# A decoder layer's down projection in 32 steps over a sliding range of contraction pairs

## The chip, the cores and the metric

The kernel runs on one core of a Trainium2 chip. The metric is the device time of one execution in microseconds (us). The kernel before took 3311.81 us (median of 3 runs, 3308.32 to 3328.85).

A core has a matrix engine (TensorE, PE in the profile, with its weight loads as PEld), VectorE (DVE), ScalarE (ACT), GpSimd (POOL) and SyncE (SP). SP here only issues DMAs; ACT and POOL issue some as well. Each engine takes its own instructions in order, and engines wait for one another by semaphores.

## The reference: what is computed

One layer of a hybrid decoder for 592 tokens (64 sample tokens, 16 meta tokens, 512 prompt tokens), D_MODEL 2048, all in float32:

```python
h = rmsnorm(x, norm1_w)
mix = token_mixer(h, ...)            # w_in projection, two groups of recurrent heads, w_out projection
x = x + mix
u = relu(rmsnorm(x, norm2_w) @ w_up) # 2048 -> 8192
x = x + (u * u) @ w_down             # 8192 -> 2048
y = rmsnorm(x, final_norm_w)
```

The change touches the last product alone, `(u * u) @ w_down`, for the 576 tokens that are returned (the meta tokens are dropped before it).

## The kernel before, in words

**Split numbers.** Every float32 operand is split into a high part (rounded to the matrix engine's fast float32 form by an ACT copy) and a low part (the rest, by a DVE subtraction). A product is three matrix products: high weights by high data, high by low, low by high.

**Seven products in place of eight.** The two MLP projections take the 576 tokens as 2 halves of TH = 288, output columns as pairs of 128-wide tiles and contraction rows as pairs. One 2 by 2 by 2 block product is made from 7 products (`FORMS`) of sums and differences of the four blocks of each side. A *pair* p is a pair of output tiles with 7 products, each over KP = 8 contraction pairs with 3 matmuls apiece: 24 matmuls of 288 columns per product, 168 per pair. The up projection has 32 pairs (p = 0 to 31), the down projection another 32 (p = 32 to 63).

**The data side of the down projection.** The squared activations of up pair q are contraction pair q of the down projection. They and their sums and differences (8 planes of 128 by 288) are made in `ub`, stored by GpSimd to the DRAM tensor `u_forms` (`store_u`, L762), and later read back. Only 8 contraction pairs fit on chip: `forms_a` (forms 0 to 2) and `forms_b` (forms 3 to 6) hold a high and a low part of each form for 8 contraction pairs.

**Four chunks.** The down projection therefore runs in 4 chunks of 8 contraction pairs. In each chunk all 8 output pairs are visited; each visit reads the output's running sum `z` from DRAM, adds its 7 products (`take`, L2180) and stores it again (`store_z`, L767). Ahead of each chunk all 7 forms are loaded anew: ACT issues one DMA of 1152 KB per form (`form_load`, L1587), turns it into the high part (`chunk_hi`, L1592) and DVE makes the low part in two halves (`chunk_lo`, L2227). This is spread over the slots of the pair before the chunk and the chunk's first pair.

**The order of the work.** It is written out by hand. Each engine runs through slots (p, i), i = 0 to 6. In slot i, DVE first adds a finished product (`take` of product i-2), then makes the low part of the weights of product i (`mlp_lo`, L2172), and in slots 1, 3, 5 and 6 one weight sum (`weight_sum`, L2137; those of slots 5 and 6 are for the next pair). ACT makes the high part of the weights of product i+1 (`mlp_hi`, L1538). TensorE waits at the head of product i for the low part of its weights (`product_waits`, L1187).

**The weights.** A pair needs 4 weight blocks of 512 KB (j = 0 to 3). SP issues them in order (`load_block`, L524) into a ring of 6, each when its place comes free; the running sums `z` go through the same queue (`load_z`, L543). Blocks 2 and 3 of a pair are needed first: the sum of the two is what DVE makes in slot 5 of the pair before. The fourth block (j = 3) is issued after the weight sum of slot 3, two slots ahead of that.

Of the kernel before, what the change touches and what calls it, by code (L numbers as in the profile page):

```python
# [21 lines left out]
F32 = mybir.dt.float32  # L22
# [6 lines left out]
P = 128  # L29
# [39 lines left out]
UB = [0, 4, 6, 3, 5, 2, 7]  # L69
BLOCK_AT = [2, 3, 0, 1, 4, 5]  # L70
DVE_FORMS = list(range(FORMS))
# [31 lines left out]
def next_form_chunk(p):  # L103

    return (p + 1 - UP_PAIRS) // KP if p + 1 >= UP_PAIRS and (p + 1 - UP_PAIRS) % KP == 0 and p + 1 < PAIRS else None

def this_form_chunk(p):
    return (p - UP_PAIRS) // KP if p >= UP_PAIRS and (p - UP_PAIRS) % KP == 0 else None
# [79 lines left out]
def hymba_kernel(nc, io):  # L189
    ctx = ExitStack()  # L190
    with ctx:
# [10 lines left out]
        u_dram = nc.dram_tensor("u_forms", [CHUNKS, FORMS + 1, P, KP, TH], F32, kind="Internal").ap()  # L202
# [106 lines left out]
        with ExitStack() as s:  # L309
# [10 lines left out]
            sb("plane_rest", [P, KP * TH - UK * P - 4 * TH], stack=s)  # L320
            with ExitStack() as s2:
                ub = sb("ub", [P, 2, FORMS + 1, TH], stack=s2)
            with ExitStack() as s2:
                z = sb("z", [P, 2, 4, TH], stack=s2)
                zsq = sb("zsq", [P, 2, TN], stack=s2)
                zacc = sb("zacc", [P, TN], stack=s2)
                fin = sb("fin", [P, NW], stack=s2)
            sb("ub_rest", [P, 2, FORMS + 1, TH], stack=s)
            w_raw2 = sb("w_raw2", [P, 2, UK, P], stack=s)

# [88 lines left out]
        s_fraw = [sem(f"form_loaded{i}") for i in range(FORMS)]  # L419
        s_tc = sem("product_copied")  # L420
# [41 lines left out]
        def _(sp):  # L462
# [61 lines left out]
            def load_block(n):  # L524
# [52 lines left out]
        def _(pool):  # L577
# [184 lines left out]
            def store_u(p):  # L762
                pool.wait_ge(s_uf, 3 * p + 3)
                pool.dma_start(u_dram[p // KP][:, :, p % KP, :].rearrange("f p n -> p f n"),
                               ub[:, p % 2]).then_inc(s_ust[p % 2], 16)

            def store_z(p):  # L767
# [3 lines left out]
                else:  # L771
                    e = d - KP * (CHUNKS - 1)
                    for r in range(2):
                        pool.wait_ge(s_zq, 2 * e + r + 1)
                        if e == 0 and r == 0:
                            pool.tensor_copy(zacc[:, :], zsq[:, 0, :]).then_inc(s_zacc, 1)
                        else:
                            pool.wait_ge(s_zacc, 2 * e + r)
                            pool.tensor_tensor(zacc[:, :], zacc[:, :], zsq[:, r, :], ALU.add).then_inc(s_zacc, 1)
# [51 lines left out]
        def _(pe):  # L831
# [341 lines left out]
            def part_product(p, i, ks):  # L1173
# [3 lines left out]
                out = pbank(p, "abacaba"[i])  # L1177
                for k in ks:
                    if p == 0 and i < 3:
                        pe.wait_ge(s_flo, form_no(f"{i}_{k}"))  # L1180
                    for n, (w, x) in enumerate(((hi_slot(u_), f_hi), (hi_slot(u_), f_lo), (w_lo[:, u_ % 2], f_hi))):
                        ins = mm(out, w[:, k, :], x[:, k, :], start=i in (0, 1, 3) and k == 0 and n == 0,  # L1182
# [4 lines left out]
            def product_waits(p, i):  # L1187
# [75 lines left out]
        def _(act):  # L1263
# [274 lines left out]
            def mlp_hi(p, i):  # L1538
# [5 lines left out]
                else:  # L1544
                    n_ = 4 * p + {0: 0, 3: 1, 6: 3}[i]
                    act.wait_ge(s_v[n_ % BLOCKS], 16 * (n_ // BLOCKS + 1))
# [7 lines left out]
            def copy_product(p, n):  # L1554

                i, dst = ((0, 0), (1, 2), (2, 1))[n]
# [8 lines left out]
            def u_square(p, n):  # L1565
# [6 lines left out]
                A(ub[:, p % 2, 2 * n:2 * n + 2, :], part[:, 2 * n:2 * n + 2, :], ACT.Square).then_inc(s_sqr, 1)  # L1572

            def z_finish(p, r):
# [3 lines left out]
                if e == 0 and r == 0:  # L1578
# [744 lines left out]
```

## Time and profile before

| | us |
|---|---|
| runs: median (lowest, highest) | 3311.81 (3308.32, 3328.85) |
| profiled execution, whole | 3322.78 |
| its span, first to last instruction | 3321.2 |
| TensorE busy | 3040.7 (92%) |
| VectorE busy | 2014.2 (61%) |
| ScalarE busy | 1189.7 (36%) |
| starts of the first and last matmul of the up and down products (L1182) | 1762.6 and 3299.2 |

The mean granted clock of TensorE was 0.96 of full speed. The page divides the span into 40 slices of 83 us; the MLP starts in slice 22. A row of the chain of waits gives a start, a length and the work that held up the end at that moment; a row of the timeline gives start, length, engine, line and operation, and in brackets the idle time before it and what ended it.

### The profile page before, as it was taken

Reading aid. Unit: us, or ns where it says so; the run is one execution under the profiler, and the core shown is the slowest. Engines: PE = TensorE matmul, PEld = TensorE weight load, DVE = VectorE, ACT = ScalarE, POOL = GpSimd, SP = SyncE. Lnnn points to the kernel's source line nnn. Section 1 sums busy time; section 2 is a strip of 40 time slices with the busy share of each in tenths; the row PEclk is TensorE's granted clock in tenths of the full one; section 3 lists DMA queues with packets and bytes.
Section 4 is the critical chain, followed back from the end, with each engine's and each line's share of the span. In section 5 each row is a group of like instructions: output and inputs, shape, how many; then the busy total and the mean of one; then the engine's idle time right before and its main releaser. Section 6 shows DMA issues by size and latency. Waiting matters only on the chain.

```text
span 3321.2 us, 54780 instructions
## 1 busy us (share of the span) xinstructions
PE 3040.7 (92%) x22024; PEld 2973.4 (90%) x22024; DVE 2014.2 (61%) x2800; ACT 1189.7 (36%) x1481; POOL 315.5 (9%) x432
## 2 busy tenths in 40 slices
PE   5999999898989898986999999999998989899798
PEld 4998988898989898875999999999997979899798
DVE  3546363645454463644447777777768777677775
ACT  3333232232323232332334444444443343333443
POOL 4010101010201011010110000000000000000021
PEclk8999999999999999997999999999999989999999
DMA  7544334542344457952433444444465565645655
GB/s 163 75 66 68 61 71 53 57 74 56 70 64 68 63 67 55 68 107 65 126 108 104 153 153 139 153 153 146 139 210 159 150 205 150 208 140 150 204 146 178
DMA packets 481058, 385.65 MB, mean 116 GB/s; under 512 B 15296, under 2 KB 446992, under 8 KB 477216
## 3 DMA queue, kind: packets, MB, share of 16 engines
q1 hardware_dynamic: 453936, 260.60, 39.2%
q0 software_dynamic: 22832, 88.39, 7.4%
q10 hardware_dynamic: 4032, 33.03, 2.6%
q8 instruction: 184, 3.01, 0.4%
q14 instruction: 74, 0.61, 0.1%
HBM read 297.65 MB, written 84.33 MB: 115 GB/s over the span
## 4 chain that ended last, share of the span: by engine, by line
PE 77%; DVE 10%; issue 6%; ACT 4%; DMA 2%; SPq 0%; DVEq 0%; POOL 0%; ACTq 0%
PE main L1182 34%; PE main L839 26%; PE mx L1182 6%; PE mx L1084 2%; PE mx L983 1%; PE mx L991 1%; PE mx L915 1%; PE mx L899 1%; DVE w_lo L2178 1%; DVE w_lo L1677 1%; DVE forms_b L2231 1%; DMA w_raw<-in_w_in 1%; ACT w_hi L1277 1%; DMA w_raw<-in_w_down 1%; PE mx L942 1%
## 5 line engine op out<-in xcount | busy, mean ns | idle before, releaser
L839 PE MATMUL main<-h_hi,w_hi 128*128 128x296 f32 (+1 forms) x2592 | 627.7, 324 | 81.7 <-DVE w_lo L1677 47.3
L1182 PE MATMUL main<-forms_b,w_hi 128*128 128x288 f32 x3072 | 624.7, 298 | 57.3 <-DVE w_lo L2178 43.1
L1182 PE MATMUL main<-forms_a,w_hi 128*128 128x288 f32 x3072 | 619.3, 297 | 14.6 <-DVE forms_a L2231 10.6
L839 PE MATMUL main<-h_lo,w_hi 128*128 128x296 f32 (+1 forms) x2592 | 579.5, 306 | 0.0
L839 PE MATMUL main<-h_hi,w_lo 128*128 128x296 f32 (+1 forms) x2592 | 577.2, 305 | 0.0
L1182 PEld LDWEIGHTS main<-forms_b,w_hi 128*128 128x128 f32 x3072 | 500.4, 191 | 60.8 <-DVE w_lo L2178 44.7
L839 PEld LDWEIGHTS main<-h_hi,w_hi 128*128 128x128 f32 x2592 | 429.8, 197 | 97.2 <-issue 52.3
L1182 PEld LDWEIGHTS main<-forms_a,w_hi 128*128 128x128 f32 x3072 | 498.0, 190 | 16.8 <-issue 16.6
L1182 PE MATMUL main<-forms_a,w_lo 128*128 128x288 f32 x1536 | 457.2, 298 | 0.0
L1182 PE MATMUL main<-forms_b,w_lo 128*128 128x288 f32 x1536 | 456.8, 297 | 0.0
L839 PEld LDWEIGHTS main<-h_lo,w_hi 128*128 128x128 f32 x2592 | 436.6, 196 | 0.0
L839 PEld LDWEIGHTS main<-h_hi,w_lo 128*128 128x128 f32 x2592 | 435.6, 195 | 0.0
L1552 ACT ACTIVATE w_hi<-w_raw 128x1024 fp32r<-128x1024 f32 x256 | 271.2, 1059 | 387.0 <-PE main L1182 251.2
L2178 DVE TENSOR_TENSOR w_lo<-w_raw,w_hi 128x1024 fp32r<-128x1024 f32 x256 | 312.3, 1220 | 65.3 <-PE main L1182 65.3
L1552 ACT ACTIVATE w_hi<-w_sum 128x1024 fp32r<-128x1024 f32 x190 | 201.4, 1060 | 340.6 <-PE main L1182 304.1
L1182 PEld LDWEIGHTS main<-forms_b,w_lo 128*128 128x128 f32 x1536 | 293.7, 191 | 0.0
L1182 PEld LDWEIGHTS main<-forms_a,w_lo 128*128 128x128 f32 x1536 | 291.0, 189 | 0.0
L1677 DVE TENSOR_TENSOR w_lo<-w_raw,w_hi 128x1024 fp32r<-128x1024 f32 x162 | 197.5, 1220 | 141.4 <-ACT w_hi L1272 97.3
L2178 DVE TENSOR_TENSOR w_lo<-w_sum,w_hi 128x1024 fp32r<-128x1024 f32 x190 | 233.8, 1231 | 16.6 <-PE main L1182 16.6
L1182 PE MATMUL mx<-forms_b,w_hi 128*128 128x288 f32 x1024 | 209.7, 298 | 8.0 <-DVE forms_b L2231 8.0
L1277 ACT ACTIVATE w_hi<-w_raw 128x1024 fp32r<-128x1024 f32 x112 | 117.8, 1052 | 241.3 <-PE main L839 241.3
L2191 DVE TENSOR_TENSOR z<-z,main 128x288 f32<-128x288 f32 x192 | 87.0, 453 | 144.7 <-PE main L1182 144.5
(375 smaller groups left out, 3715.1 us busy)
## 6 DMA issues: line engine op xcount, KB each, us to landing
w_raw<-in_w_in SPq DMA_DIRECT2D x130, 512.0 KB, 8.3
w_raw<-in_w_up SPq DMA_DIRECT2D x128, 512.0 KB, 4.0
w_raw<-in_w_down SPq DMA_DIRECT2D x128, 512.0 KB, 4.7
u_forms<-ub POOLq DMA_DIRECT2D x32, 1152.0 KB, 6.6
forms_b<-u_forms ACTq DMA_DIRECT2D x16, 1152.0 KB, 7.7
z<-x_scratch SPq DMA_DIRECT2D x32, 576.0 KB, 7.6
x_scratch<-z POOLq DMA_DIRECT2D x31, 576.0 KB, 3.1
w_raw<-in_w_out SPq DMA_DIRECT2D x32, 512.0 KB, 4.2
```

The costliest lines, as they stand in the source:

```text
L839: ins = mm(out[:, half, :], w[:, ring, k, :], x[:, kx, half * width:half * width + width], start=first and n == 0, stop=last_ and n == 2)
L899: ins = mm(mx[:, i + half, 0:HALF], ones[:, :], src[:, half * HALF:half * HALF + HALF], start=True, stop=True)
L915: ins = pe.transpose(mxf[:, 512 * i + n_ * P:512 * i + n_ * P + P], src(c), ident[:, :])
L942: ins = mm(mx[:, 2 * i + half, 0:HALF], ones[0:16, :], sel[i][:, half * HALF:half * HALF + HALF], start=True, stop=True)
L983: ins = mm(bank(0, 64 * c, 64), xl[:, c, :], left, start=True, stop=True)
L1084: ins = mm(bank(i % 2, 64 * c, 64), win(hkk, c), hqq[:, ctok(c):ctok(c) + 64], start=True, stop=True)
L1182: ins = mm(out, w[:, k, :], x[:, k, :], start=i in (0, 1, 3) and k == 0 and n == 0, stop=k == KP - 1 and n == 2, skip_group_check=True)
L1277: A(w_hi[:, ring % 2], w_raw[:, ring], ACT.Copy).then_inc(s_hi, 1)
L1552: A(hi_slot(u_), src, ACT.Copy).then_inc(s_hi, 1)
L1677: TT(w_lo[:, ring % 2], w_raw[:, ring], w_hi[:, ring % 2].bitcast(F32), ALU.subtract).then_inc(s_lo, 1)
L2178: TT(w_lo[:, u_ % 2], src, hi_slot(u_).bitcast(F32), ALU.subtract).then_inc(s_lo, 1)
L2191: TT(o[:, q, :], o[:, q, :], src, ALU.add).then_inc(s_ev, 1)
```

## The change

The down projection is no longer in 4 chunks but in 32 steps t = 0 to 31. Step t still makes the 7 products of output pair t mod 8 over 8 contraction pairs, but these are t to t+7, taken modulo 32. So each output pair is visited 4 times, and its four ranges together cover all 32 pairs once. From one step to the next a single contraction pair leaves the range and one comes in. Its 7 forms (3 for `forms_a`, 4 for `forms_b`) overwrite the place of the one that left.

- The first fill (7 forms of 8 pairs) is issued by SP (`load_form`), among the weight blocks, no longer by ACT.
- The other three fills of all forms are gone. Each of steps 1 to 31 has two loads issued by ACT (`step_load`: 3 planes, then 4 planes), into a buffer `stage` (for step 1 straight into the forms), two ACT copies for the high parts (`step_hi`), and two DVE subtractions for the low parts (`step_lo`).
- TensorE waits for them in the middle of a product: in products 0 and 3 of a step, ahead of the last of the 8 contraction pairs.
- `u_forms` is stored by contraction pair, so that the 3 planes and the 4 planes each lie together; the planes in `ub` have another order for it, and with them some slices of ACT and DVE in the up projection.
- From step 25 on the range wraps round, and a weight block is loaded by two DMAs in place of one.
- `zsq` and `zacc` move onto `part` and `rstd` to make room for `stage`.

```diff
@@ sync (SP) @@
-                    c, m = (p - UP_PAIRS) // KP, 2 * ((p - UP_PAIRS) % KP) + j // 2
-                    src = w_down[:, KT * c + j % 2:KT * c + KT:2, m * P:m * P + P]
+                    m = 2 * ((p - UP_PAIRS) % KP) + j // 2
+                    q, i = window(p)[0], 0
+                    while i < KP:
+                        n_ = min(KP - i, UP_PAIRS - q)
+                        src = w_down[:, 2 * q + j % 2:2 * (q + n_ - 1) + j % 2 + 1:2, m * P:m * P + P]
+                        sp.dma_start(wblock(n)[:, i:i + n_, :], src).then_inc(s_v[n % BLOCKS], 16)
+                        q, i = 0, i + n_
+                    return
...
+            def load_form(i):
+
+                sp.wait_ge(s_unit, unit_of(UP_PAIRS - 1, i) + 1)
+                sp.wait_ge(s_ust[0], 16 * (KP // 2))
+                sp.wait_ge(s_ust[1], 16 * (KP // 2))
+                sp.dma_start(form(i)[1].bitcast(F32), u_dram[0:KP, UB[i]].rearrange("k p n -> p k n")).then_inc(s_fraw[i], 16)
...
+                for i in {4 * UP_PAIRS + 2: (0, 1), 4 * UP_PAIRS + 4: (2,)}.get(n, ()):
+                    load_form(i)
                 if p >= UP_PAIRS:
                     load_z(p)
+                for i in {4 * UP_PAIRS + 4: (3, 4), 4 * UP_PAIRS + 5: (5, 6)}.get(n, ()):
+                    load_form(i)
@@ tensor (PE) @@
+                t = p - UP_PAIRS
                 for k in ks:
+                    if t > 0 and k == KP - 1 and i in (0, 3):
+                        pe.wait_ge(s_flo, step_forms(t, i // 3))
...
+                    kx = k if t < 0 else window(p)[k] % KP
...
-                c = this_form_chunk(p)
-                if c is not None:
-                    if i in DVE_FORMS:
-                        pe.wait_ge(s_flo, len(F_ORDER) + len(DVE_FORMS) * c + DVE_FORMS.index(i) + 1)
+                if p == UP_PAIRS:
+                    pe.wait_ge(s_flo, len(F_ORDER) + i + 1)
@@ scalar (ACT) @@
-            def form_load(c, i):
-                act.wait_ge(s_ust[0], 16 * (KP // 2) * (c + 1))
-                act.wait_ge(s_ust[1], 16 * (KP // 2) * (c + 1))
-                act.dma_start(form(i)[1].bitcast(F32), u_dram[c, UB[i]]).then_inc(s_fraw[i], 16)
...
+            def step_load(t, group):
+
+                q = (t + KP - 1) % UP_PAIRS
+                i0, i1 = (4, 8) if group else (0, 3)
+                act.wait_ge(s_ust[q % 2], 16 * (q // 2 + 1))
+                src = u_dram[q, i0:i1].rearrange("f p n -> p f n")
+                if t == 1:
+                    dst = (forms_b if group else forms_a)[:, :, 1, q % KP, :].bitcast(F32)
+                else:
+                    dst = stage[:, i0:i1, :]
+                    if t == 2:
+                        act.wait_ge(s_ust[1], 16 * (UP_PAIRS // 2))
+                    else:
+                        act.wait_ge(s_flo, step_forms(t - 1, group))
+                act.dma_start(dst, src).then_inc(s_step[group], 16)
+
+            def step_hi(t, group):
...
+                act.wait_ge(s_step[group], 16 * t)
+                act.wait_ge(s_unit, unit_of(UP_PAIRS + t - 1, 6 if group else 2) + 1)
+                A(f[:, :, 0, q, :], f[:, :, 1, q, :].bitcast(F32) if t == 1 else stage[:, i0:i1, :], ACT.Copy).then_inc(s_fhi, 1)
...
+                if t > 1 and i == 1:
+                    step_hi(t, 1)
+                if 0 < t < STEPS - 1:
+                    if i == 0:
+                        step_load(t + 1, 0)
+                    if i == 3:
+                        step_load(t + 1, 1)
+                    if i == 4:
+                        step_hi(t + 1, 0)
@@ vector (DVE) @@
+            def step_lo(t, group):
+                q = (t + KP - 1) % KP
+                f = forms_b if group else forms_a
+                dve.wait_ge(s_fhi, step_forms(t, group))
+                lo_ = f[:, :, 1, q, :]
+                TT(lo_, lo_.bitcast(F32) if t == 1 else stage[:, 4:8, :] if group else stage[:, 0:3, :],
+                   f[:, :, 0, q, :].bitcast(F32), ALU.subtract).then_inc(s_flo, 1)
...
+                if t > 1 and i == 2:
+                    step_lo(t, 1)
+                if 0 < t < STEPS - 1 and i == 4:
+                    step_lo(t + 1, 0)
```

**SP's queue at the first fill.** These are SP's DMAs from the blocks of the first down pair on (L541 or L562: a weight block; L551 or L582: a running sum; L572: one form of the fill), before:

```order
L541 DMA w_raw<-in_w_down 128x8x128 [waits weights_lo] x2
L541 DMA w_raw<-in_w_down 128x8x128 [waits weight_sum_made] x2
L541 DMA w_raw<-in_w_down 128x8x128 [waits weights_lo]
L551 DMA z<-x_scratch 128x1152 [waits x1_stored1,x1_stored0,u_stored0]
L541 DMA w_raw<-in_w_down 128x8x128 [waits weights_lo]
L541 DMA w_raw<-in_w_down 128x8x128 [waits weight_sum_made] x2
```

and now:

```order
L562 DMA w_raw<-in_w_down 128x8x128 [waits weights_lo] x2
L562 DMA w_raw<-in_w_down 128x8x128 [waits weight_sum_made]
L572 DMA forms_a<-u_forms 128x8x288 [waits u_stored1,u_stored0,unit_done] x2
L562 DMA w_raw<-in_w_down 128x8x128 [waits weight_sum_made]
L562 DMA w_raw<-in_w_down 128x8x128 [waits weights_lo]
L572 DMA forms_a<-u_forms 128x8x288 [waits u_stored1,u_stored0,unit_done]
L582 DMA z<-x_scratch 128x1152 [waits x1_stored1,x1_stored0,u_stored0]
L572 DMA forms_b<-u_forms 128x8x288 [waits u_stored1,u_stored0,unit_done] x2
L562 DMA w_raw<-in_w_down 128x8x128 [waits weights_lo]
L572 DMA forms_b<-u_forms 128x8x288 [waits u_stored1,u_stored0,unit_done] x2
L562 DMA w_raw<-in_w_down 128x8x128 [waits weight_sum_made] x2
```

The fourth block of the first down pair now stands behind two forms, and the third and fourth block of the second down pair behind all seven; before, no form was in this queue.

**DVE in one step of the new down projection** (slots 2 to 5 of a step; L2255 adds a product, L2242 makes a low part of weights, L2233 and L2216 are weight sums, L2304 is `step_lo`):

```order
L2255 TENSOR_TENSOR z<-z,main 128x288 [waits z_loaded0,unit_done]
L2242 TENSOR_TENSOR w_lo<-w_sum,w_hi 128x1024 [waits unit_done,weights_hi]
L2304 TENSOR_TENSOR forms_b<-stage,forms_b 128x4x288 [waits form_hi]
L2255 TENSOR_TENSOR z<-z,main 128x288 [waits unit_done]
L2242 TENSOR_TENSOR w_lo<-w_raw,w_hi 128x1024 [waits unit_done,weights_hi]
L2233 TENSOR_TENSOR w_sum<-w_raw,w_sum 128x1024 [waits weights_lo,weight_sum_made,block_loaded1]
L2255 TENSOR_TENSOR z<-z,main 128x288 [waits unit_done]
L2242 TENSOR_TENSOR w_lo<-w_raw,w_hi 128x1024 [waits unit_done,weights_hi]
L2304 TENSOR_TENSOR forms_a<-stage,forms_a 128x3x288 [waits form_hi]
L2255 TENSOR_TENSOR z<-z,mx 128x288 [waits product_taken,unit_done]
L2242 TENSOR_TENSOR w_lo<-w_sum,w_hi 128x1024 [waits unit_done,weights_hi]
L2216 TENSOR_TENSOR w_sum<-w_raw 128x1024 [waits weight_sum_made,weights_lo,block_loaded1,block_loaded0]
```

The two subtractions stand in slots 2 and 4, the slots of the down projection that had no weight sum besides slot 0. Apart from them a step has the same DVE instructions as a pair inside a chunk had.

## Rows read from the trace of the kernel before

**Rows 1.** The page: busy time by engine

```profile
PE 3040.7 (92%) x22024; PEld 2973.4 (90%) x22024; DVE 2014.2 (61%) x2800; ACT 1189.7 (36%) x1481; POOL 315.5 (9%) x432
```

**Rows 2.** Chain of waits, 2440 to 3321 us: start, length, work

```profile
2452.12 3.20 PE mx L1182 x24
...
2546.27 3.20 PE mx L1182 x24
...
2657.75 3.21 PE mx L1182 x24
...
2748.82 3.22 PE mx L1182 x24
...
2860.32 3.19 PE mx L1182 x24
...
2953.02 3.19 PE mx L1182 x24
...
3064.54 3.19 PE mx L1182 x24
...
3153.00 3.19 PE mx L1182 x24
...
3286.80 3.20 PE mx L1182 x24
```

**Rows 3.** Timeline of DVE, 2455 to 2545 us

```profile
2456.85 1.22 DVE L2152 TENSOR_TENSOR w_sum<-w_raw 128x1024 f32<-128x1024 f32 x1
...
2458.55 0.45 DVE L2201 TENSOR_TENSOR part<-part,main 128x288 f32<-128x288 f32 x1 [0.47 <-PE main L1182]
...
2478.00 1.22 DVE L2178 TENSOR_TENSOR w_lo<-w_sum,w_hi 128x1024 fp32r<-128x1024 f32 x1
2493.81 1.23 DVE L2152 TENSOR_TENSOR w_sum<-w_raw 128x1024 f32<-128x1024 f32 x1 [14.60 <-issue]
...
2495.32 1.22 DVE L2178 TENSOR_TENSOR w_lo<-w_raw,w_hi 128x1024 fp32r<-128x1024 f32 x1
...
2524.24 1.22 DVE L2152 TENSOR_TENSOR w_sum<-w_raw 128x1024 f32<-128x1024 f32 x1
...
2533.45 1.21 DVE L2178 TENSOR_TENSOR w_lo<-w_raw,w_hi 128x1024 fp32r<-128x1024 f32 x1
2536.76 0.45 DVE L2191 TENSOR_TENSOR z<-z,main 128x288 f32<-128x288 f32 x1 [2.10 <-PE main L1182]
```

**Rows 4.** SP: timeline from 2470 us; landing of L541's DMA issued 2471 to 2475

```profile
2473.70 2.43 SPq L541 DMA_DIRECT2D w_raw<-in_w_down  x2
...
DMA to landing us min/median/max: 20.0/20.0/20.0
```

**Rows 5.** Timeline of DVE, then of ACT, inside a chunk, 2562 to 2586 us

```profile
2565.39 0.45 DVE L2191 TENSOR_TENSOR z<-z,main 128x288 f32<-128x288 f32 x1 [1.57 <-PE main L1182]
...
2571.78 0.46 DVE L2191 TENSOR_TENSOR z<-z,mx 128x288 f32<-128x288 f32 x1 [1.53 <-PE mx L1182]
...
2568.65 1.07 ACT L1552 ACTIVATE w_hi<-w_sum 128x1024 fp32r<-128x1024 f32 x1 [2.14 <-PE main L1182]
```

**Rows 6.** All uses of L2231, then of the copies L1595: min/median/max in ns

```profile
L2231 DVE TENSOR_TENSOR forms_b<-forms_b x32: 1346/1349/1354, 2515.3 to 3138.5; 128x1152 fp32r<-128x1152 f32 x32
...
L1595 ACT ACTIVATE forms_b<-forms_b x16: 2107/2115/2125, 2504.3 to 3124.9; 128x2304 fp32r<-128x2304 f32 x16
```

**Rows 7.** One pair by engine (busy PE, PEld, DVE, ACT, POOL; clock, DMA share, GB/s)

```profile
2562.30:2584.60 22.30, 22.30 (x171) 22.30 (x170) 15.77 (x19) 7.47 (x8) 0.53 (x1) 1.00 0.51 148
```

**Rows 8.** DMA issues in 2570 to 2592 us: KB each, median us to landing

```profile
w_raw<-in_w_down SPq DMA_DIRECT2D x4, 512.0 KB, 4.8
```

**Rows 9.** Landing of all 28 form loads, L1590

```profile
DMA to landing us min/median/max: 5.1/9.3/12.1
```

**Rows 10.** DMA totals in 1560 to 1580 us, then in 1568 to 1576 us

```profile
DMA packets 7726, 5.48 MB, mean 274 GB/s; under 512 B 2025, under 2 KB 7662, under 8 KB 7726
...
DMA packets 3241, 2.71 MB, mean 339 GB/s; under 512 B 832, under 2 KB 3241, under 8 KB 3241
```

More of the change, by code:

```diff
@@ L100, in out_done, with window, block_loads, block_count @@
     return OUT_U0 + (3 + m if m < 2 else 2 * m + 2)
[L103 to L109, printed above, removed]
+STEPS = PAIRS - UP_PAIRS
+FIRST_FORMS = len(F_ORDER) + FORMS
+def window(p):
+    return [(p - UP_PAIRS + i) % UP_PAIRS for i in range(KP)]
+def block_loads(n):
+    p = n // 4
+    return 2 if p >= UP_PAIRS and p - UP_PAIRS + KP > UP_PAIRS else 1
+def block_count(n):
+    return 16 * sum(block_loads(m) for m in range(n % BLOCKS, n + 1, BLOCKS))
+def step_forms(t, group):
+    return FIRST_FORMS + 2 * (t - 1) + 1 + group
 def w0(c):
@@ L324, in hymba_kernel @@
                 z = sb("z", [P, 2, 4, TH], stack=s2)
-                zsq = sb("zsq", [P, 2, TN], stack=s2)
-                zacc = sb("zacc", [P, TN], stack=s2)
-                fin = sb("fin", [P, NW], stack=s2)
+                stage = sb("stage", [P, FORMS + 1, TH], stack=s2)
             sb("ub_rest", [P, 2, FORMS + 1, TH], stack=s)
             w_raw2 = sb("w_raw2", [P, 2, UK, P], stack=s)
+        zsq = part[:, :, :].rearrange("p (a b) n -> p a (b n)", a=2)
+        zacc = rstd[:, 0:TN]
         def x1_tile(m):
@@ L419, in hymba_kernel @@
         s_fraw = [sem(f"form_loaded{i}") for i in range(FORMS)]
+        s_step = [sem(f"step_forms_loaded{i}") for i in range(2)]
         s_tc = sem("product_copied")
@@ L1571, in u_square @@
                         act.wait_ge(s_ust[p % 2], 16 * (p // 2))
-                A(ub[:, p % 2, 2 * n:2 * n + 2, :], part[:, 2 * n:2 * n + 2, :], ACT.Square).then_inc(s_sqr, 1)
+                A(ub[:, p % 2, (4 if n else 0):(7 if n else 4):(2 if n else 3), :], part[:, 2 * n:2 * n + 2, :], ACT.Square).then_inc(s_sqr, 1)
             def z_finish(p, r):
@@ L1577, in z_finish @@
                 act.wait_ge(s_ev, ev_no(p, 6 + r))
-                if e == 0 and r == 0:
-                    act.wait_ge(s_ust[1], 16 * (UP_PAIRS // 2))
                 if e:
@@ L1609, in slot @@
                         z_finish(p - 1, i)
[L1610 to L1621 removed]
+                t = p - UP_PAIRS
+                if t == -1 and i >= 5:
+                    chunk_hi(i - 5)
+                if t == 0 and i < 5:
+                    chunk_hi(i + 2)
+                if t == 0 and i == 4:
+                    step_load(1, 0)
+                if t == 0 and i == 6:
+                    step_hi(1, 0)
+                if t == 1 and i == 1:
+                    step_load(1, 1)
+                if t == 1 and i == 2:
+                    step_hi(1, 1)
+                if t > 1 and i == 1:
[7 more added lines that the diff above has]
+                        step_hi(t + 1, 0)
             mlp_hi(0, 0)
@@ L2200, in take @@
                     dve.wait_ge(s_tc, 3 * p + 2)
[L2201 removed]
+                    TT(part[:, 3, :], part[:, 3, :], a, ALU.add).then_inc(s_ev, 1)
                 elif i == 5:
@@ L2248, in slot @@
                     u_forms(p - 1, i // 2 - 1)
-                c = next_form_chunk(p)
-                if c is not None and i == 6:
-                    chunk_lo(c, 0, 0)
-                c = this_form_chunk(p)
-                if c is not None:
-                    for f, half in {0: [(0, 1)], 1: [(1, 0), (1, 1)], 2: [(2, 0), (2, 1)], 3: [(3, 0), (3, 1)], 4: [(4, 0), (4, 1)],
-                                    5: [(5, 0), (5, 1)], 6: [(6, 0), (6, 1)]}[i]:
-                        chunk_lo(c, f, half)
+                t = p - UP_PAIRS
+                if t == -1 and i == 6:
+                    chunk_lo(0, 0)
+                if t == 0:
+                    for f, half in {0: [(0, 1)], 1: [(1, 0), (1, 1)], 2: [(2, 0), (2, 1)], 3: [(3, 0), (3, 1)],
+                                    4: [(4, 0), (4, 1)], 5: [(5, 0), (5, 1)], 6: [(6, 0), (6, 1)]}[i]:
+                        chunk_lo(f, half)
+                if t == 1 and i == 0:
+                    step_lo(1, 0)
+                if t == 1 and i == 3:
+                    step_lo(1, 1)
+                if t > 1 and i == 2:
+                    step_lo(t, 1)
+                if 0 < t < STEPS - 1 and i == 4:
+                    step_lo(t + 1, 0)
             weight_sum(0, 1)
```

57 lines of the change are left out of this document (23 added, 34 removed).

## The prediction

> **What bounds the kernel now.** First the page's busy times [rows 1]: TensorE is busy 92% of the span, DVE 61%, ACT 36%. Little is to be had except where TensorE stands still. Then the chain of waits over the down projection [rows 2]. The rows "PE mx x24" are product 3 of a pair, one per pair, so their starts are a clock with one tick per pair. Inside the last chunk six pairs pass between 3153.00 and 3286.80: 22.30 us per pair, which is 168 matmuls at 0.133. At this pace TensorE is never idle [rows 7], and no edit here makes it faster. Across a chunk's start the clock jumps. Each of these intervals holds three pairs, 66.90 us at full pace:
>
> - start of chunk 0, 2452.12 to 2546.27: 94.15, so 27.25 lost
> - chunk 1, 2657.75 to 2748.82: 91.07, 24.17 lost
> - chunk 2, 2860.32 to 2953.02: 92.70, 25.80 lost
> - chunk 3, 3064.54 to 3153.00: 88.46, 21.56 lost
>
> Together 98.8 us; that is all the change can win from this stage, since the rest of it runs at full pace.
>
> What the loss consists of is read from DVE's timeline at chunk 0 [rows 3]. In a normal pair the weight sum for the next pair (L2152) follows the low part before it without a gap (2456.85). At chunk 0 it should have started when the low part ended (2478.00 + 1.22 = 2479.2) and started at 2493.81: 14.60 us idle. It needed the fourth weight block, which SP issued at 2473.70 and which took 20.0 us to land [rows 4]; blocks in the middle of a chunk take 4.8 [rows 8]. In those 20 us ACT's form loads were running. From then on DVE has no idle mark at all. From the low part at 2495.32 to the one of the same work eight products later, 2533.45, are 38.13 us; TensorE needs 8 x 3.19 = 25.5 for them. So 12.6 us go to DVE's extra work, 14 subtractions of 1.35 us [rows 6], and 14.6 + 12.6 = 27.2 is the whole loss. Two parts: **a late weight block, and DVE too full in a chunk's first pair.**
>
> **The change part by part.**
>
> *Three refills go.* Chunks 1 to 3 no longer start. Their 24.17 + 25.80 + 21.56 = 71.5 us go, unless the work that takes their place is late in each step (next points).
>
> *Work of a step on DVE.* Two subtractions, of 4 x 288 = 1152 elements (1.35 us [rows 6]) in slot 2, and of 3 x 288 = 864 elements in slot 4 (1152 take 1.35 and 1024 take 1.22 [rows 6, 3], so 864 about 1.05). In these slots DVE now idles 1.57 and 1.53 us [rows 5], so both fit, with 0.2 and 0.5 to spare. DVE goes from 15.8 to 18.2 of 22.3 us per step. If one runs over by some tenths, the next low part is later by as much, and that costs nothing up to 1.6 us: the low part that ended at 2479.2 was for product 5 of its pair, due at 2452.12 + 22.30 + 2 x 3.19 = 2480.8.
>
> *Work of a step on ACT.* Two copies: 2304 elements take 2.11 us and 1024 take 1.07 [rows 6, 5], so 1152 and 864 about 1.16 and 0.92. ACT idles 2.14 us in a slot [rows 5]. In the last 8 pairs it has squares in slots 0 and 1 as well; 1.07 + 1.45 + 1.16 is 0.5 over one slot, made up in the next. One thing is tight: in slot 4 the copy comes behind the weights' copy (1.07 + 0.92 = 2.0 us after product 2 ends), and DVE's subtraction behind it, 2.0 + 1.05 = 3.05 of 3.19. That still fits.
>
> *Loads of a step.* They are issued four and five slots (12.8 and 16 us) ahead of their copies; form loads twice as large and more took 5.1 to 12.1 [rows 9]. Covered. The exception is step 1, where the loads come two slots and one slot ahead: ACT waits some us there, which its slack and the wait's place (last contraction pair of a product) take up.
>
> *What the loads do to the weights.* A step now moves 7 x 128 x 1152 bytes = 1.03 MB more, on 148 GB/s x 22.3 us = 3.3 MB [rows 7]: 194 GB/s, where 274 to 339 were reached [rows 10]. What counts is the fourth block, the one that was late. It has 5.5 us from issue (2473.70) to its use (2479.2), and DVE's 0.47 us of idle [rows 3] and the 1.6 us above come on top: TensorE is hit from about 7.5 us on. It takes 4.8, and behind the four planes of a step (0.59 MB at 339 GB/s = 1.7 us) at worst 6.5. I book nothing.
>
> *The first fill.* DVE's part stays: the same 14 subtractions stand in the same slots, 12.6 us. Of the other 14.6 us the change can win between all and little. All of it, if forms and blocks in one queue do not hold each other up. For the other end I let a block wait for all that was issued before it. The fourth block (issued 2473.70) then waits for one block and two forms, the first of them issued two slots earlier, at 2467.3: 0.52 + 1.18 + 1.18 + its own 0.52 = 3.4 MB. At 339 GB/s that is 10.0 us, at 274 it is 12.4 [rows 10]; the fixed part is 3.3 us (the 4.8 of rows 8 less 0.52 MB at 339). So it lands at 2480.6 or 2483.0, which is 1.0 or 3.4 us after 2479.2 and the idle 0.47. Blocks 3 and 4 of the second pair wait for all seven forms: 7 x 1.18 + 6 x 0.52 + 0.59 (a running sum) + 1.18 (a store of u) = 13.2 MB, 38.9 or 48.2 us, landing at 2509.5 or 2518.8. DVE would ask for them 14.6 us ahead of 2524.24 [rows 3], at 2509.6: 0 or 9 us late, less what was lost already, so 0 or 6 more. Between 14.6 and 14.6 - 9.4 = 5 us are won; I take 10, nearer to the 339 GB/s that SP's queue reached when it was full.
>
> *TensorE's 62 new waits* (two per step, 31 steps). Satisfied waits at product heads cost nothing visible: six products in a row keep 22.30 us per pair. Zero, at most one matmul pitch each, 62 x 0.13 = 8 us.
>
> *The rest.* Split weight blocks in the last 7 steps: 28 DMAs more on SP, which is idle between them. Re-ordered planes in the up projection: same sizes. Moved scratch tiles: no work. Nothing.
>
> **Sum:** 71.5 + 10 = 81.5 us. The profiled execution took 3322.78 us, which gives 3241.3. It lies 11.0 above the median of the runs, 3311.81; on that base the sum gives 3230.3. I say 3230.
>
> **The rivals.**
>
> 1. *The first fill is no better than before*: the forms ahead of blocks on SP's queue cost what ACT's queue cost. For it: seven forms ahead of two blocks DVE needs, and SP's wait for a store of u (at the running sum) with forms 3 to 6 behind it. Against: only two forms stand ahead of the block that was late. Then 71.5 alone is won, 3240; with 3 us more lost, 3243. Chance 0.17.
> 2. *Each step loses about a microsecond*: the chain ACT copy, DVE subtraction in slot 4 uses 3.05 of 3.19 us, slot 2 uses all but 0.2, and both run on strided planes, which no row times. Against: the 1.6 us of lead. 31 x 1 us: 3261. Chance 0.10.
> 3. *Slower: the fourth block is late in every step.* Step loads go through ACT's queue, the one whose loads made a block take 20.0 us. If the block took as long as the slowest form load did (12.1 us [rows 9]) TensorE would stand 12.1 - 7.5 = 4.6 us in each of 31 steps, 143 us, and 3311.8 - 81.5 + 143 = 3373. It decides from 7.5 + 81.5 / 31 = 10.1 us of landing. Against it: a step brings 1.03 MB in two parts, where a refill brought 8.3 MB within two pairs. Chance 0.05.
> 4. *The change does not do what it says*, since a step's forms are ready only after the last contraction pair is reached, so that the wait moves into every step. The slots speak against it: forms a are made in slot 4 of the step before and used three products later, forms b in slot 2 and used at the end of product 3. It would look like rival 2 or 3; 0.02.
>
> The forecast keeps 0.66.
>
> **The numbers.** A measurement of this kernel tells about 1%, 33 us, from no change: faster means under 3279. That holds the forecast, rival 1 and most of rival 2: 0.92. Within 1%: 0.04. Slower than 3345: 0.04. The range goes down to a first fill that wins all of 14.6 us, on the lowest run: 3308.3 - 86.1 = 3222, and 6 us for the spread of the runs, 3216. Up it takes in rival 1 (3243), the 8 us of TensorE's waits and a share of rival 2: 3256.
>
> **What would show it.** The starts of product 3 should tick at 22.3 us from the second step to the last, across steps 8, 16 and 24 too. At the first step one jump of 13 to 22 us should be left, with DVE without idle marks. DVE should be busy about 18.2 us per step. The fourth block should land within 7 us. Ticks of 23 us or more in every step would be rival 2 (DVE without idle) or rival 3 (DVE idle ahead of L2216); a jump of 27 at the first step would be rival 1.

## The result, and the profile after

| us | before | after |
|---|---|---|
| median (lowest, highest), 4 runs each | 3318.01 (3308.32, 3328.85) | 3238.51 (3236.98, 3238.73) |
| profiled execution | 3322.78 | 3238.73 |
| its span | 3321.2 | 3237.2 |

The ratio is 0.9765 (95% interval 0.9746 to 0.9783): 2.35% faster, about 78 us; the medians are 79.5 us apart. The forecast was 3230 with a range of 3216 to 3256. Two further series of the changed kernel gave medians of 3237.02 and 3240.71 us, ratios 0.9768 (0.9743 to 0.9793) and 0.9785 (0.9772 to 0.9799). Beside before in the same series (3311.60 and 3310.76) these are 74.6 and 70.1 us less, so the gain lies between 70 and 80 us.

The page after answers to [rows 1]. DVE has 21 us more work, the matrix engine 11 less busy time, in a span 84.0 us shorter:

```profile
PE 3029.5 (94%) x22024; PEld 2966.3 (92%) x22024; DVE 2035.5 (63%) x2820; ACT 1204.8 (37%) x1522; POOL 318.1 (10%) x432
```

The chain of waits of after answers to [rows 2]: start, length, work, and one "mx x24" per pair.

```profile
2444.29 3.20 PE mx L1220 x24
...
2531.35 3.20 PE mx L1220 x24
2534.55 19.10 PE main L1220 x144
2553.65 3.19 PE mx L1220 x24
...
3201.08 3.19 PE mx L1220 x24
```

Between product 3 of step 1 (2531.35) and product 3 of step 31 (3201.08) lie 30 steps: 669.73 us, 22.324 each. No refill is left. The one jump is the first fill, 87.06 us for three pairs, so 20.16 over the 66.90 of full pace.

With the marks of before, the 84.0 us of span split up as follows:

| part | before | after | won |
|---|---|---|---|
| all stages ahead, to product 3 of the last up pair but one | 2452.12 | 2444.29 | 7.8 |
| first fill, over three pairs at 22.30 | 27.25 | 20.16 | 7.1 |
| three refills | 71.53 | 0 | 71.5 |
| 30 steps at 22.324, not 22.30 | | | -0.7 |
| last product 3 to the end of the span | 34.40 | 36.12 | -1.7 |

The first row is not put down to the change. The 7.8 us are there already at product 3 of up pair 1 (1797.57 against 1805.40), right behind the start of the MLP. The mark of the first row lay at 2441.57 to 2445.28 in the three profiles of the changed kernel. Of the kernels below that differ from it only in the down projection, one has it at 2443.70 and the six others at 2449.83 to 2454.24. What moves it stays open. Without it the change is worth 76.2 us in these two traces, and 77.9 without the tail, which varies too (last section).

The timeline of DVE after, at the first fill, answers to [rows 3] (start, length, line, operation, in brackets the idle time before it):

```profile
2470.17 1.22 DVE L2242 TENSOR_TENSOR w_lo<-w_sum,w_hi 128x1024 fp32r<-128x1024 f32 x1
2477.99 1.23 DVE L2216 TENSOR_TENSOR w_sum<-w_raw 128x1024 f32<-128x1024 f32 x1 [6.60 <-issue]
...
2481.76 1.35 DVE L2295 TENSOR_TENSOR forms_a<-forms_a 128x1152 fp32r<-128x1152 f32 x1
```

The same weight sum as in [rows 3] is still late, by 6.60 us and no longer 14.60. Its block stands in SP's queue behind two forms. The timeline of SP, and the landing of the block issued at 2465.87:

```profile
2460.30 3.47 SPq L572 DMA_DIRECT2D forms_a<-u_forms  x2
2465.87 4.55 SPq L562 DMA_DIRECT2D w_raw<-in_w_down  x2
...
DMA to landing us min/median/max: 12.0/12.0/12.0
```

The steady step, 2710.00 to 2732.30 us, answers to [rows 7] (us; busy PE, PEld, DVE, ACT, POOL; clock, DMA share, GB/s). The timeline of DVE in it shows the two new subtractions, the DMA issues answer to [rows 8]:

```profile
2710.00:2732.30 22.30, 22.30 (x170) 22.30 (x169) 18.04 (x20) 9.30 (x9) 0.53 (x1) 1.00 0.64 193
```

```profile
2711.94 1.06 DVE L2304 TENSOR_TENSOR forms_a<-stage,forms_a 128x864 fp32r<-128x864 f32 x1 [0.31 <-ACT forms_a L1649]
...
2727.46 1.35 DVE L2304 TENSOR_TENSOR forms_b<-stage,forms_b 128x1152 fp32r<-128x1152 f32 x1
```

```profile
w_raw<-in_w_down SPq DMA_DIRECT2D x4, 512.0 KB, 4.9
...
stage<-u_forms ACTq DMA_DIRECT2D x1, 576.0 KB, 3.9
stage<-u_forms ACTq DMA_DIRECT2D x1, 432.0 KB, 4.4
```

TensorE is busy throughout, DVE 18.04 us (forecast 18.2), and the blocks land in 4.9 us beside the step loads.

### The profile page after: what moved, and what is told of

It is laid out like the page before. It is cut to its first block, busy times and chain, and to the rows that moved or that the text cites. A ratio compares the mean times of both kernels' runs of the same rounds, so it can differ in the third digit from the quotient of the medians.

```text
span 3237.2 us, 55001 instructions
## 1 busy us (share of the span) xinstructions
PE 3029.5 (94%) x22024; PEld 2966.3 (92%) x22024; DVE 2035.5 (63%) x2820; ACT 1204.8 (37%) x1522; POOL 318.1 (10%) x432
## 4 chain that ended last, share of the span: by engine, by line
PE 82%; DVE 7%; issue 5%; ACT 4%; DMA 1%; SPq 1%; DVEq 0%; POOL 0%; ACTq 0%
PE main L1220 37%; PE main L873 26%; PE mx L1220 6%; PE mx L1118 2%; PE mx L1017 1%; PE mx L1025 1%; PE mx L949 1%; PE mx L933 1%; DVE w_lo L1741 1%; ACT w_hi L1313 1%; DMA w_raw<-in_w_in 1%; PE mx L976 1%; PE mx L1059 0%; ACT tmp L1473 0%; PE mx L1135 0%
## 5 line engine op out<-in xcount | busy, mean ns | idle before, releaser
L1220 PE MATMUL main<-forms_b,w_hi 128*128 128x288 f32 x3072 | 617.4, 296 | 7.7 <-DVE w_lo L2242 5.4
L2242 DVE TENSOR_TENSOR w_lo<-w_raw,w_hi 128x1024 fp32r<-128x1024 f32 x256 | 312.3, 1220 | 65.3 <-PE main L1220 65.3
L2242 DVE TENSOR_TENSOR w_lo<-w_sum,w_hi 128x1024 fp32r<-128x1024 f32 x190 | 234.1, 1232 | 16.6 <-PE main L1220 16.6
L1220 PEld LDWEIGHTS mx<-forms_b,w_hi 128*128 128x128 f32 x1024 | 165.4, 189 | 2.7 <-issue 2.7
```

The lines of the kernel that those rows point to most:

```text
L1220: ins = mm(out, w[:, k, :], x[:, kx, :], start=i in (0, 1, 3) and k == 0 and n == 0, stop=k == KP - 1 and n == 2, skip_group_check=True)
L2242: TT(w_lo[:, u_ % 2], src, hi_slot(u_).bitcast(F32), ALU.subtract).then_inc(s_lo, 1)
```

## The experiments

The refills and the steps agree with the prediction at once, the first fill does not in its makeup. The theory after the result: the gain there comes from the move out of ACT's queue, and what is left is the fourth block behind two forms. The rival: it comes from the shorter rows in DRAM. `u_forms` is now laid out by contraction pair, so a form of the fill is read in rows of 288 numbers, 1152 bytes, where a chunk's form had rows of 8 x 288 numbers, 9216 bytes. The prediction had put this change of layout down as work that moves nothing.

**The changed kernel again**, without any edit, for the spread of the marks.

> The changed kernel once more, as the measure for the others of this call. Expected: within 0.3% of 3238.5 us; at the start of the down projection DVE idle about 6.6 us ahead of its sum L2216; three pairs across it 87 us; 22.32 us per step after it.

3237.02 us (3235.91 to 3240.04); three pairs 87.10 us, DVE idle 6.62 us.

**The fill back on ACT's queue, the rest of the change kept.**

```diff
-                for i in {4 * UP_PAIRS + 2: (0, 1), 4 * UP_PAIRS + 4: (2,)}.get(n, ()):
-                    load_form(i)
...
+                if t == -1 and i >= 2:
+                    load_form(i - 2)
+                if t == 0 and i < 2:
+                    load_form(i + 5)
```

> The changed kernel with one part undone: ACT issues the seven forms of the first fill, in the slots in which it did before; SP's queue holds blocks and running sums alone. Rows in DRAM stay 1152 bytes long (before: 9216). Theory A (a load on ACT's queue starves SP's blocks, whatever its rows): the fourth block lands after about 20 us again, DVE idles 14.6 us, the three pairs across the start take 94 us, the kernel 7 us more than the changed one, about 3246. Theory B (engines take turns packet by packet, so the length of the rows on ACT's queue decides): with 1152 against 512 bytes the block's 0.52 MB goes through with 1.2 MB of forms and some of the store of u, 5 to 7 us at 340 GB/s plus 3.3 fixed: it lands after 8 to 10 us, DVE idles 3 to 5 us, less than the 6.6 of SP's queue, and the kernel takes 2 to 4 us less than the changed one.

3238.50 us (3234.03 to 3242.28), three pairs 2443.70 to 2531.55, 87.85. The block issued at 2465.3 took 13.7 us, and DVE waited 8.29:

```profile
2479.09 1.23 DVE L2221 TENSOR_TENSOR w_sum<-w_raw 128x1024 f32<-128x1024 f32 x1 [8.29 <-issue]
```

Theory A fell: back on ACT's queue the fill costs 0.8 us more and not 7. Theory B (the row length decides) is nearer, since the block took 13.7 us and not 20.0, but it too was off: it had 8 to 10 us, a wait of 3 to 5, and a kernel 2 to 4 us faster than the changed one.

**Before, with only the first fill moved to SP's queue**, its long rows kept.

```diff
+            def load_form(i):
...
+                sp.dma_start(form(i)[1].bitcast(F32), u_dram[0, UB[i]]).then_inc(s_fraw[i], 16)
...
+                for i in {4 * UP_PAIRS + 2: (0, 1), 4 * UP_PAIRS + 4: (2,)}.get(n, ()):
+                    load_form(i)
...
+                for i in {4 * UP_PAIRS + 4: (3, 4), 4 * UP_PAIRS + 5: (5, 6)}.get(n, ()):
+                    load_form(i)
...
-                    if i >= 2:
+                    if i >= 2 and c:
...
-                    if i < 2:
+                    if i < 2 and c:
```

> The kernel before with one part of the change alone: the first of its four fills issued by SP at the places the change gives it, with the rows of the kernel before (9216 bytes). The other three fills stay on ACT's queue. Theory A (bytes ahead in one queue): 3.4 MB ahead of and with the block at 340 to 420 GB/s, so it lands after 8.5 to 12 us and DVE idles 3 to 6.6 us at chunk 0 where it idled 14.6; chunks 1 to 3 lose 21 to 26 us each as before; the kernel gains 8 to 11 us on the kernel before, most of it within its spread. Rival (form loads in flight starve blocks in either queue): idle about 14.6 at chunk 0, no gain.

3307.99 us (3303.56 to 3317.62), ratio 0.999 (0.9975 to 1.0006), which by itself shows nothing; the marks in the trace do. Three pairs 2449.77 to 2535.64, 85.87: 18.97 lost and not 27.25. The block took 11.8 us, DVE waited 6.32. So with long rows the move of the queue wins 8.3 us.

**Before, with only the short rows**, all four fills left on ACT's queue.

```diff
-        u_dram = nc.dram_tensor("u_forms", [CHUNKS, FORMS + 1, P, KP, TH], F32, kind="Internal").ap()
+        u_dram = nc.dram_tensor("u_forms", [UP_PAIRS, FORMS + 1, P, TH], F32, kind="Internal").ap()
...
-                act.dma_start(form(i)[1].bitcast(F32), u_dram[c, UB[i]]).then_inc(s_fraw[i], 16)
+                act.dma_start(form(i)[1].bitcast(F32), u_dram[KP * c:KP * c + KP, UB[i]].rearrange("k p n -> p k n")).then_inc(s_fraw[i], 16)
```

> The kernel before in everything (its chunks, its four fills, all on ScalarE's queue) but for the layout of the forms in DRAM: rows of 1152 B instead of 9216 B in the fills. Theory (the row length of the competing load decides how long a weight block takes, as the fill on ScalarE's queue in rows of 1152 B suggests): VectorE's idle time at chunk 0 falls from 14.6 to about 8.3 us, chunk 0 costs about 21 us over its pace instead of 27.25, chunks 1 to 3 about 17 to 19 each instead of 24.2, 25.8 and 21.6, and the kernel is 20 to 25 us faster than before, near 3290 us. Rival (that gain came from something else in the change, such as form 0 being split or the next steps' smaller loads): losses as before, 3312 to 3318 us.

3288.50 us (3283.74 to 3298.62) beside 3316.55 of before, ratio 0.993 (0.9907 to 0.9953): a layout won 28 us by the medians, 23 (15 to 31) by the ratio. The chain of waits, to be held against [rows 2]:

```profile
2450.28 3.19 PE mx L1181 x24
2537.40 3.19 PE mx L1181 x24
...
2648.88 3.21 PE mx L1181 x24
2731.01 3.21 PE mx L1181 x24
...
2842.51 3.19 PE mx L1181 x24
2897.77 4.96 PE mx L1181 x24
2926.31 3.19 PE mx L1181 x24
...
3037.83 3.19 PE mx L1181 x24
3119.85 3.20 PE mx L1181 x24
```

Less 66.90 each, the four chunks lose 20.2, 15.2, 16.9 and 15.1 us, where before lost 27.25, 24.17, 25.80 and 21.56: 31.3 us in all, somewhat more than the theory had. At chunk 0 the block took 13.0 us, not 20.0, and DVE waited 7.54, not 14.60. The DMA totals over 2470 to 2490 us show how (packets, MB, share of the DMA engines; q10 is ACT's queue, q1 SP's). Before:

```profile
q10 hardware_dynamic: 677, 5.65, 68.1%
q1 hardware_dynamic: 1589, 0.80, 16.1%
```

With short rows:

```profile
q10 hardware_dynamic: 4097, 4.65, 68.9%
q1 hardware_dynamic: 2348, 1.41, 23.9%
```

The packets of ACT's queue shrink from 8.3 KB (5.65 MB / 677) to 1.1 KB, and the weights, in packets of 0.5 to 0.6 KB, get 1.41 MB through in the same 20 us and not 0.80. Both kernels move much the same in all (7.66 and 7.27 MB). The ratio of bytes between the two queues falls from 7.1 to 3.3. It doesn't fall as far as the sizes of the packets do. The Trainium skill (DMA: Bandwidth & Descriptors, section Queues, rings and completion order) says that a DMA engine changes between queues only at the end of a packet, and that a packet there typically holds some 9 to 17 descriptors. The trace agrees in direction if the profile's packets stand for these, which no run here shows. The edit changes the addresses in DRAM along with the row length, for the stores of `u` too, and no run parts the two; that the packets got shorter at much the same total rate speaks for the row length.

**The changed kernel, forms 0 and 1 behind the fourth block.**

```diff
-                for i in {4 * UP_PAIRS + 2: (0, 1), 4 * UP_PAIRS + 4: (2,)}.get(n, ()):
+                for i in {4 * UP_PAIRS + 3: (0, 1), 4 * UP_PAIRS + 4: (2,)}.get(n, ()):
```

> The changed kernel with forms 0 and 1 of the first fill issued behind the fourth block of the first down pair in place of ahead of it. Theory A (a block waits for the bytes issued ahead of it in its own queue): nothing is ahead of the block, it lands after about 5 us, the 6.6 us of idle time on DVE go but for 1 us, since the forms then arrive 5.5 us later, which ACT's copy of form 0 just bears; the kernel gains 5 to 6 us, about 3233. Rival (the 12 us came from the store of u, or the forms delay DVE instead): the block still takes 9 us or more, or DVE idles as long ahead of its first subtraction L2295; no gain.

3234.91 us (3230.10 to 3241.01); three pairs 85.57, so 1.5 us won and not 5 to 6. The block landed after 6.7 us and DVE's wait ahead of the weight sum fell to 1.24 us, so the two forms ahead of it did hold it up, but a new one came at the first low part of a form, since form 0 was now issued late:

```profile
2486.41 1.36 DVE L2295 TENSOR_TENSOR forms_a<-forms_a 128x1152 fp32r<-128x1152 f32 x1 [4.25 <-ACT forms_a L1624]
```

**TensorE's new waits at the heads of products 0 and 3** rather than ahead of their last contraction pair.

```diff
-                    if t > 0 and k == KP - 1 and i in (0, 3):
-                        pe.wait_ge(s_flo, step_forms(t, i // 3))
...
+                if p > UP_PAIRS and i in (0, 3):
+                    pe.wait_ge(s_flo, step_forms(p - UP_PAIRS, i // 3))
```

> The changed kernel with TensorE's waits for a step's forms moved from the middle of products 0 and 3 to their heads, where other waits stand. The forms are ready there (low parts of forms 3 to 6 end in slot 2). If the wait in the middle of a product breaks its pipeline, the pace goes from 22.324 us per step back to the 22.30 of the kernel before: 0.7 us over 30 steps. If the 0.024 us have another cause (SBUF places, steps' DMAs), it stays.

3238.81 us (3232.39 to 3242.82); 22.324 us per step, as with the waits inside. In the middle of a product the waits cost nothing that can be seen. The 0.024 us per step over 22.30 is left without a cause. At the heads they do cost something in one place, product 3 of step 1:

```profile
2537.13 3.43 PE mx L1218 x24
2540.56 19.10 PE main L1218 x144
2559.66 3.19 PE mx L1218 x24
```

TensorE stands 1.02 us ahead of this product for `step_lo` of forms 3 to 6, and the product takes 3.43 us; in the changed kernel, with the wait inside, the same product took 3.20 with no such wait. The 1.02 us are in the figure for three pairs (87.30), the other 0.23 behind it. The same holds for the next two kernels, which keep the waits at the heads.

**The same (waits at the heads), with form 0 ahead of the fourth block and form 1 behind it.**

```diff
-                for i in {4 * UP_PAIRS + 2: (0, 1), 4 * UP_PAIRS + 4: (2,)}.get(n, ()):
+                for i in {4 * UP_PAIRS + 2: (0,), 4 * UP_PAIRS + 3: (1,), 4 * UP_PAIRS + 4: (2,)}.get(n, ()):
```

> As e6, and SP issues form 0 ahead of the fourth block and form 1 behind it (the changed kernel has both ahead, e2 had both behind). By bytes ahead in the queue: when the block is issued about 0.8 MB of form 0 are still to come, so it lands after 7 us and DVE idles 1.5 us ahead of its sum L2216 (6.6 in the changed kernel, 1.2 in e2); form 0 lands as early as in the changed kernel, so that the 4.25 us that DVE stood in e2 ahead of its first subtraction do not come. Three pairs across the start take 81.5 to 83 us (87.1 in the changed kernel, 85.6 in e2, 79.5 if only DVE's work were left); the kernel gains 4 to 6 us on the changed one, about 3233.

3236.67 us (3229.18 to 3241.37), in each of four rounds 1.5 to 3.2 us under the kernel with only the waits moved; 4 to 6 had been forecast against the changed kernel. Three pairs 83.04 us, not 87.30:

```profile
2480.46 1.23 DVE L2216 TENSOR_TENSOR w_sum<-w_raw 128x1024 f32<-128x1024 f32 x1 [1.00 <-issue]
```

One form of 1.18 MB less ahead of the block takes 5.6 us off DVE's wait, and the block lands after 6.4 us and not 12.0. The section of the Trainium skill named above also has descriptors of one ring consumed in order; this row agrees.

**The same, with the work on the first forms half a form earlier** (ACT's copy of form 0 one slot, each of DVE's 14 subtractions).

```diff
-                if t == -1 and i >= 5:
-                    chunk_hi(i - 5)
+                if t == -1 and i in (4, 6):
+                    chunk_hi(i // 2 - 2)
...
-                if t == -1 and i == 6:
-                    chunk_lo(0, 0)
+                if t == -1 and i >= 5:
+                    chunk_lo(0, i - 5)
...
```

> The same as the run before it (waits at the heads, form 0 ahead of the fourth block, form 1 behind it, all on SP's queue), with the work on the first forms moved half a form earlier: ScalarE copies form 0 already in slot 4 of step 31, and each of VectorE's fourteen subtractions of the first fill stands half a form earlier, the first in slot 5 of step 31, the last in slot 6 of step 32. Theory (VectorE's saturated stretch sets the loss): it begins one slot earlier and uses that slot's free 0.45 to 1.3 us, so the three pairs take 81.7 to 82.6 us instead of 83.04, and the kernel 0.5 to 1.3 us less. Rival (the landing of the forms sets it now; ScalarE waited 4.24 and 3.18 us for forms 1 and 2): no gain, 82.8 to 84 us.

3233.86 us (3233.41 to 3243.41), three pairs 82.30 (81.7 to 82.6 forecast). The theory held in the trace; the whole times of the two kernels come from different series.

**This version and the changed kernel, round by round.**

> The changed kernel once more, beside the version with the earlier low parts: 3235 to 3240 us, three pairs at the first step 87.1 us.

> The version with form 0 ahead of the fourth block, form 1 behind it, TensorE's waits at the heads and the low parts half a form earlier, measured round by round beside the changed kernel. Theory (what the trace's clock shows, 87.1 against 82.3 us for the three pairs, comes out in the whole time): 4 to 5.5 us less than the changed kernel in the mean over the rounds. Rival (the stages ahead and the tail, which differ by some us from run to run, cover it or take it back): less than 2 us between them.

Medians 3234.75 (3231.75 to 3239.31) and 3240.71 us (3233.48 to 3242.15). By round the difference is +5.8, -7.9, -2.6, -0.6 and -10.3, -3.1 in the mean: between the theory and the rival, and smaller than its own spread. Three pairs took 81.57 and 86.13 us, so 4.6 are won at the first step, 4.3 with the pair behind it. But in these two profiles the mark ahead of the down projection came 9.3 us later in this version (2450.89 against 2441.57), so that its profiled execution was the slower one, 3239.31 against 3233.48 us: what varies ahead of the MLP is larger than what is won. Over all series 9 runs of this version have a mean of 3235.9 and 13 of the changed kernel 3238.2, 2.3 apart with a standard error of 1.4. In the trace it is the better kernel; in the whole time that isn't shown.

**How full DVE may be.** Two kernels give DVE more to do in steps 2 to 22. The first repeats the two subtractions of a step into scratch memory:

```diff
+                if 1 < t < 23:
+                    if group:
+                        TT(part[:, :, :], src_, hi_, ALU.subtract)
+                    else:
+                        TT(px, src_, hi_, ALU.subtract)
```

> The changed kernel with DVE work doubled in steps 2 to 22: beside each of the step's two subtractions a second one of the same kind, whose result is written to PSUM or to a scratch tile and used by nobody. DVE's demand rises by about 2.2 us to 20.2 of 22.3 us per step; slot 2 then holds 4.1 us and slot 4 3.5 us of work where a slot of TensorE is 3.19. Theory (low parts are made 1.5 us ahead, so a slot may run over by that much as long as the step's sum fits): 22.3 us per step in these steps too, no more than 2 us on the whole kernel. Rival (each slot must fit by itself, so that the change was within 0.2 us of losing in every step): 0.9 + 0.3 = 1.2 us more per step, 25 us over 21 steps.

3244.33 us in one run, 22.325 us per step. No loss, and so 1.5 us of lead do even out slots of which single ones run over (slot 2 took DVE 4.04 us, 2621.77 to 2625.81, where TensorE's slot is 3.19):

```profile
2620.00:2642.30 22.30, 22.30 (x170) 22.30 (x170) 19.84 (x23) 9.28 (x10) 0.53 (x1) 1.00 0.65 190
```

The second adds another two subtractions of 3 planes and two of 2 planes.

> As the one before, with three idle subtractions beside each of the two, in steps 2 to 22: DVE's demand is about 23.5 us per step, over the 22.3 that TensorE needs. Theory (the step's sum on DVE is what decides): 23.5 to 24.5 us per step in these steps, 25 to 45 us on the whole kernel, and 22.3 again from the first step without them. It gives the price of a microsecond of DVE work per step beyond the edge.

3309.63 us in one run: the steps in question took 25.4 us (2818.18 to 3072.45 is 254.27 for ten). That is 3.1 us more per step where 1.2 to 2.2 had been expected:

```profile
2840.00:2865.40 25.40, 22.84 (x170) 22.37 (x170) 23.05 (x27) 9.36 (x10) 0.54 (x1) 1.00 0.57 171
```

DVE's own work, 23.05 us, would ask for 0.75 more than 22.30; the other 2.3 us are gaps, 2.35 of 25.40 in which DVE waits: 1.44 and 0.46 for a product of TensorE, ahead of its work in slots 1 and 2, and 0.44 for an ACT copy. The direction held, the size did not: DVE's work summed over a step is not the whole price once it is over the edge.

## Why the prediction came out as it did

**The refills, 71.5 us: right.** They are gone, and nothing late took their place at steps 8, 16 and 24. But of the 71.5 some 24 hung on the long rows (8.9, 8.9 and 6.4 us of the three losses go with the layout alone). With short rows, the kernel before stands at 3288.5 us, and the change wins about 50 us over that, not 79.5.

**The work of a step, nothing: right.** The subtractions took 1.35 and 1.06 us (forecast 1.35 and 1.05), ACT's copies 1.15 and 0.91 (1.16 and 0.92), the loads landed in 3.9 and 4.4 us, the blocks in 4.9 (at most 6.5). The pace of 22.324 costs 0.7 us over the whole. Rivals 2, 3 and 4 fell. TensorE's 62 waits, put at nothing, cost nothing where the change has them. The kernel with 1.8 us more on DVE and no loss shows that rival 2 was further off than its tight slots made it look.

**The first fill, 10 us: the step that was off.** 7.1 were won. Three things were off in it.

- *The count of bytes.* The prediction had the block wait for 3.4 MB and land after 6.9 to 9.3 us; it took 12.0. The DMA totals of after over 2458 to 2478 us, the 20 us until it landed, show 1.18 MB beside them, the GpSimd queue's store of u. The prediction had counted it for the later blocks only:

```profile
DMA packets 5592, 5.32 MB, mean 266 GB/s; under 512 B 93, under 2 KB 5334, under 8 KB 5590
...
q1 hardware_dynamic: 5318, 4.11, 69.4%
q0 software_dynamic: 272, 1.18, 15.6%
```

  At 339 or 274 GB/s these are 3.5 or 4.3 us, and 6.9 to 9.3 becomes 10.4 to 13.6. This is an estimate: no run leaves the store out. SP's own queue moved 4.08 MB from the issue of the first form (2460.30) to the landing, 0.7 more than the 3.4 that stood ahead of or in the block, so loads issued behind it took a share as well.
- *The later blocks.* The low end of 5 us came from blocks 3 and 4 of the second pair. DVE had no idle time ahead of their sum, so nothing was lost:

```profile
2509.24 1.22 DVE L2216 TENSOR_TENSOR w_sum<-w_raw 128x1024 f32<-128x1024 f32 x1
```

- *The cause of the gain.* The prediction gave it to the queue. Each edit alone wins about the same, the short rows 7.0 us and SP's queue 8.3, and both together no more, 7.1 to 8.0 (86.13 to 87.10 us for the three pairs). On ACT's queue long rows crowd out the weights; on SP's the block waits for what stands ahead of it. Within the change, the queue is worth 0.8 to 1.7 us. The prediction's last term has "Re-ordered planes in the up projection: same sizes" among what costs and gains nothing, and says no word of the rows of the fill: that was wrong, and it hid what the kernel before with short rows gained, 23 to 28 us.

That the size came out near is partly luck. Since each edit takes away much the same wait, leaving one of them out of the account did not show in the sum. For the changed kernel with its fill on ACT's queue the same reasoning would have forecast no gain at the first fill; it won 6.3 us (94.15 to 87.85).

The jump of 13 to 22 us was there, 20.2, but not "with DVE without idle marks". That sign did not fit the prediction's own sum: a win of 10 of the 14.6 us leaves 4.6 of idle time. Rival 1 (the fill no better) fell, by 7 us.

**The whole.** The sum of 81.5 stood against 76.2 in these two traces; the rest of their 84.0 was there when the up projection began. The forecast on the median was 3230, and 3238.5, 3237.0 and 3240.7 were measured. All three lie in the range. 3 us of the 8 are the fill, 2.4 the pace and the tail of the profiled execution. The remainder lies within the spread of the runs, of before too: the forecast started from its median over 3 runs, 3311.81, and later series gave 3310.76 to 3316.55.

## What to carry to other kernels

When a load is late beside another queue's traffic, look at the row length of that other load as well as at its queue and its size: here short rows on the other side, or the move to the urgent load's own queue, each won 7 to 8 us by itself, and both together no more. On one queue, count every byte ahead of the urgent load and, by the estimate above, every store that runs beside it, and issue just as much ahead of it as the next consumer needs at once. A slot that ran over by itself did not matter here while the engine had a lead of 1.5 us and was 89% busy.

## What was not expected of the hardware

- Rows of 1152 bytes in place of 9216 in the loads of one queue took a 512 KB block on another from 20.0 us to 13.0 (13.7 within the change), at much the same total rate (383 and 363 GB/s).
- DVE at 89% of a step (19.84 of 22.30) cost nothing, while 23.05 us of work made the step 25.4 (one run each).
- The granted clock fell near the end of some executions. Two windows of after, and of the same place of before:

```profile
3212.00:3218.00 6.00, 6.00 (x48) 5.79 (x48) 0.45 (x1) 2.12 (x3) 0.00 (x0) 0.88 0.01 1
3218.00:3224.00 6.00, 6.00 (x33) 5.67 (x32) 1.33 (x2) 1.64 (x4) 0.00 (x0) 0.55 0.15 33
```

```profile
3298.00:3304.00 6.00, 6.00 (x56) 6.00 (x55) 0.45 (x1) 1.84 (x3) 0.00 (x0) 1.00 0.00 0
3304.00:3310.00 6.00, 5.89 (x55) 5.62 (x55) 3.84 (x3) 3.81 (x5) 0.00 (x0) 1.00 0.48 95
```

  TensorE was busy without a gap, and 0.55 is nearly all at the lower level, 1.2 GHz. The three profiles with this fall have tails of 36.1 us, nine without it 34.2 to 34.4. So the 1.7 us go with it, though the clock need not be all that sets the tail: two profiles without the fall (of the last version) have 35.4. It is not the change's: a third profile of the changed kernel has a tail of 34.27 us, as before had (34.40). What brings it on stays open.
